# The rotary part of attention's scores as three pairs of 64-row products instead of two pairs of 128-row products

## The chip, the cores and the metric

The kernel runs on one core of one Trainium2 chip. The metric is the device time of one execution in microseconds; three executions of the kernel before took 3389.27 to 3390.84 us, with a median of 3389.57 us.

## The reference, cut to what matters

Two decoder blocks follow each other over 1024 tokens of width 1024. The first has two layers (`DEPTH = 2`), each with latent attention, a convolution branch and a mixture of experts; the second block has other mixers and no such attention. The change lies in the attention of the two layers of the first block.

```
SEQ = 1024; N_ATTN_HEADS = 4; QK_NOPE_DIM = 128; QK_ROPE_DIM = 64; Q_BLOCK = 128

k_r = jnp.broadcast_to(k_rope[:, :, None, :], (B, S, N_ATTN_HEADS, QK_ROPE_DIM))
k = jnp.concatenate([k_nope, k_r], axis=-1)
q = rms_norm(q, q_head_g)
k = rms_norm(k, k_head_g)
q = jnp.concatenate([q[..., :QK_NOPE_DIM], apply_rope(q[..., QK_NOPE_DIM:], cos, sin)], axis=-1)
k = jnp.concatenate([k[..., :QK_NOPE_DIM], apply_rope(k[..., QK_NOPE_DIM:], cos, sin)], axis=-1)
def attend(q_blk):
    s = jnp.einsum('bhqd,bhkd->bhqk', q_blk, kt, preferred_element_type=jnp.float32) * scale
    p = jax.nn.softmax(s, axis=-1).astype(vt.dtype)
    return jnp.einsum('bhqk,bhkd->bhqd', p, vt)
```

A head's key has 192 numbers: 128 without position and 64 that are rotated. Scores, softmax and output are computed for blocks of 128 queries.

## The kernel before, in words

Five engines run programs written out by hand; they are ordered only by the semaphores that the code names. Each layer runs `project`, then `heads`, then `attend`, then `conv_norm_and_mix`, then the experts.

**Scores (`scores`, L1207 to L1217).** For a head and a block of 128 queries, TensorE fills two PSUM banks, one for each half of the 1024 keys (512 keys a half). Values are kept as a rounded part and a remainder (`_hi`, `_lo`), so that products can run in the faster fp32r form. The 128 position-free rows take three products for each half: high by high, high by low, low by high. The 64 rotated rows are laid out so that they fill 128 rows: `k_parts` holds the keys' high part in rows 0 to 63 and their low part in rows 64 to 127, and the queries (`qs_rope_hi`, `qs_rope_lo`) stand twice, once in each half of the rows. Two products for each half do these: the high queries with both key parts, and the low queries with both. This makes ten products of 128 rows for a call of `scores`.

**The loop (`attend`, L1243 to L1262).** There are 8 query blocks by 4 heads, 32 calls of `scores` in a layer and 64 in all. For head g TensorE turns the probabilities (8 transposes, `turn_probs`), computes the scores of head g + 2 (`scores`), and multiplies the probabilities of head g with the values (`outputs`, L1239, 8 products in plain fp32, which a trace shows as 16 records). VectorE meanwhile runs for each head the maximum over the scores (L1307), its scaling (L1309), the reciprocal of the row sum (L1314), the normalising of the probabilities (L1316), and taps of the convolution: one for each head (L1329) and a second one on every other head (L1335). ScalarE takes the exponential (L1268) and copies the turned probabilities. Two calls of `scores` stand ahead of the loop.

**The keys' rotary parts (`heads`).** In `heads` the keys of head h lie in `k_rope[:, h, :]`, the same 64 rotated rows twice. `scale_keys` on VectorE writes them. ScalarE's `rope_parts` (L923) rounds the upper 64 rows into scratch (`rope_hi` of that function, a row of `mix`) and the lower 64 rows into `k_parts`, each over 1024 keys; VectorE's `rope_low` (L976) subtracts the scratch from the upper rows. From the second head on ScalarE first waits until VectorE is done with the scratch (`rope_split`). `k_parts` lies in the same memory as `k_rope`.

**Order at the end of `heads`.** VectorE's queue holds, in this order, the scaling of the last head's keys (L973, L974), `rope_low` (L979), the splits of the position-free keys (L1016, L1018, L983), and the query scales (L1021 to L1025). ScalarE's queue holds `rope_parts`, `take` for the last query tile (L906, L907), `root` (L917) and `high` (L921). TensorE ends with products made to keep it busy (L223) and the transposes of L1056, whose moving part is 40 rows by 40 columns.

Of the kernel before, what the change touches and what calls it, by code (L numbers as in the profile page):

```python
# [13 lines left out]
F32 = mybir.dt.float32  # L14
# [118 lines left out]
def build(nc, A):  # L133
# [3 lines left out]
    with ExitStack() as top:  # L137
# [42 lines left out]
        def bank(i):  # L180
            return psum[:, i, :]
# [193 lines left out]
        def half_of(n):  # L375

            return slice(n * HALF, (n + 1) * HALF)
# [231 lines left out]
        def project(l, lcols, modl, gain, lc, shift, lat, y, mix, q):  # L609

            with ExitStack() as ctx:
# [15 lines left out]
                with nc.Block() as block:  # L627
# [137 lines left out]
                    def _(pe):  # L765
# [43 lines left out]
                        lat_spreads(1)  # L809
                        tile(conv_pairs[3], 1)  # L810

        def heads(l, lc, lat, q, y, mix):


# [4 lines left out]
            with ExitStack() as ctx:  # L819
# [6 lines left out]
                sum_rows = [slice(32 * half, 32 * half + 2 * HEADS) for half in range(2)]  # L826
                both_sums = slice(0, 32 + 2 * HEADS)
                row_roots = (mix[:, 3, 0:HALF], mix[:, 2, 0:HALF])
                rope_hi = mix[ROPE:P, 3, :].bitcast(F32R)
                cos_row = k_rope[:, HEADS - 1, :]  # L830

                rope_rows = [lat[:, 3, :], q_rope[:, 0, :], q_rope[:, 1, :]]
                names = ("w_in", "sq_done", "lat_done", "summed", "prod", "raw_done", "v_prod", "v_copied", "row_root", "root_turned", "rstd",
                         "spread_done", "q_scaled", "cos_part", "sin_part", "roped", "k_done", "rope_rounded",
                         "parts", "hi_rounded", "hi_after", "k_split", "rope_split", "conv_step")
                (w_in, sq_done, lat_done, summed, prod, raw_done, v_prod, v_copied, row_rooted, root_turned, inverted,
                 spread_done, q_scaled, cos_part, sin_part, roped, k_done, rope_rounded,
                 parts_done, hi_rounded, hi_after, k_split, rope_split, conv_step) = [sem("hd_" + n) for n in names]
                zeroed = sem("hd_zeroed")
                staged = [sem(f"hd_staged{p}") for p in range(HEADS // 2)]  # L840
                turned = [sem(f"hd_turned{n}") for n in range(3)]
# [13 lines left out]
                with nc.Block() as block:  # L855
# [43 lines left out]
                    @block.scalar  # L899
                    def _(act):  # L900
                        def take(n):
                            kind, j = tiles[n]
                            act.wait_ge(prod, n + 1)
                            if n:
                                act.wait_ge(summed, n)
                            act.activation(sq[:, (n + 1) % 2, :], banks(2 * (n % 2)), ACT.Square).then_inc(sq_done, 1)  # L906
                            act.activation(dest[kind][:, j, :], banks(2 * (n % 2)), ACT.Copy, scale=lc(gains[kind])).then_inc(raw_done, 1)  # L907

                        def copy_v(t):
                            act.wait_ge(v_prod, t + 1)  # L910
                            act.copy(v[:, t, :], bank(t % 4)).then_inc(v_copied, 1)

                        def root(i, count):
                            act.wait_ge(summed, count)
                            for half in range(2):
                                rows = sum_rows[half]
                                act.activation(row_roots[i][rows, :], bank(6 + half)[rows, :], ACT.Sqrt, bias=EPS,  # L917
                                               scale=1.0 / QK).then_inc(row_rooted, 1)

                        def high(h):  # L920
                            act.copy(k_hi[:, h, :], k_nope[:, h, :]).then_inc(hi_rounded, 1)  # L921

                        def rope_parts(i):  # L923
                            h = turn_order[i]
                            act.wait_ge(k_done, 2 * i + 2)
                            if i:
                                act.wait_ge(rope_split, i)
                            act.copy(rope_hi, k_rope[ROPE:P, h, :]).then_inc(rope_rounded, 1)
                            act.copy(k_parts[0:ROPE, h, :], k_rope[0:ROPE, h, :]).then_inc(parts_done, 1)

                        act.activation(sq[:, 0, :], lat[:, 3, :], ACT.Square).then_inc(sq_done, 1)
                        for n in range(n_k):
                            take(n)
                        root(0, 1 + n_k)
                        for t in range(TB):
                            copy_v(t)
                        rope_parts(0)
                        high(turn_order[0])
                        take(n_k)
                        rope_parts(1)  # L940
                        take(n_k + 1)
                        rope_parts(2)
                        take(n_k + 2)
                        take(n_k + 3)
                        take(n_k + 4)
                        rope_parts(3)
                        take(n_k + 5)
                        root(1, 1 + len(tiles))
                        act.wait_ge(k_done, 2 * HEADS)
                        high(turn_order[3])  # L950

                    @block.vector
                    def _(dve):
# [21 lines left out]

                        def rope_low(i):  # L976
                            h = turn_order[i]
                            dve.wait_ge(rope_rounded, i + 1)
                            dve.tensor_tensor(k_parts[ROPE:P, h, :], k_rope[ROPE:P, h, :], rope_hi.bitcast(F32), ALU.subtract).then_inc(rope_split, 1)  # L979

                        def low(h, n):
                            dve.wait_ge(hi_rounded, n)
# [137 lines left out]
        def attend(l, lc, y, mix, q):  # L1120
# [8 lines left out]
            with ExitStack() as ctx:  # L1129
# [30 lines left out]
                with nc.Block() as block:  # L1160
# [12 lines left out]
                    @block.gpsimd  # L1173
                    def _(pool):
                        def stage(pair, count, at):

                            two = slice(2 * pair, 2 * pair + 2)
                            loaded, rounded = (pool.snap(pool.to_reg(n)) for n in (64 * (count - 1), 4 * count - 2))
                            pool.tensor_copy(qs_hi[:, two, :], q_nope[:, two, at]).then_inc(staged[pair], 1)
                            pool.wait_ge(rope_loaded[pair], 64)  # L1180
                            pool.wait_ge(rope_loaded[pair], loaded)
                            pool.tensor_copy(rope_hi[:, two, :], rope_in[:, two, :]).then_inc(staged[pair], 1)
                            pool.wait_ge(staged[pair], 2)
                            pool.wait_ge(staged[pair], rounded)
                            pool.tensor_tensor(qs_lo[:, two, :], q_nope[:, two, at], qs_hi[:, two, :].bitcast(F32),
                                               ALU.subtract).then_inc(staged[pair], 1)
                            pool.tensor_tensor(rope_lo[:, two, :], rope_in[:, two, :], rope_hi[:, two, :].bitcast(F32),
                                               ALU.subtract).then_inc(staged[pair], 1)

                        for pair in range(HEADS // 2):  # L1190
                            pool.sem_inc(staged[pair], 4)
                        with pool.Fori(0, last_blk) as blk:
                            nxt = blk + 1

                            pool.wait_ge(conv_step, n_conv * blk + 1)
                            pool.wait_ge(more_step, ATTEND_MORE * blk + 1)
                            pool.tensor_copy(taps[:, 0:n_conv], lc("conv_w")[:, bass.ds(n_conv * blk + first_tap, n_conv)]).then_inc(taps_in, 1)
                            pool.tensor_copy(taps[:, n_conv:n_conv + ATTEND_MORE],
                                             lc("conv_w")[:, bass.ds(ATTEND_MORE * blk + first_more, ATTEND_MORE)]).then_inc(taps_in, 1)
                            for pair in range(HEADS // 2):  # L1200

                                pool.wait_ge(scores_done, HEADS * blk + 2 * pair + 2)
                                stage(pair, blk + 2, bass.ds(nxt * P, P))

                    @block.tensor
                    def _(pe):
                        def scores(h, slot, blk):  # L1207

                            pe.wait_ge(staged[h // 2], 4 * blk + 4)

                            parts = ((qs_hi[:, h, :], k_hi[:, h, :]), (qs_hi[:, h, :], k_lo[:, h, :]), (qs_lo[:, h, :], k_hi[:, h, :]),
                                     (rope_hi[:, h, :], k_parts[:, h, :]), (rope_lo[:, h, :], k_parts[:, h, :]))
                            for n, (queries, keys) in enumerate(parts):
                                for half in range(2):
                                    mm = pe.matmul(bank(2 * slot + half), queries, keys[:, half * HALF:(half + 1) * HALF],
                                                   start=n == 0, stop=n == len(parts) - 1)
                            mm.then_inc(scores_done, 1)  # L1217

                        for b in range(2):
                            pe.sem_inc(pv_done[b], 1)  # L1220
# [82 lines left out]
                    @block.vector  # L1303
                    def _(dve):
                        def maxima(h, slot, g, blk):
                            dve.wait_ge(scores_done, g + 1)
                            dve.reduce_max(row_max[:, slot:slot + 1], score_slot(slot), AX.X).then_inc(maxes, 1)  # L1307
                            dve.wait_ge(maxes, g + 1)
                            dve.tensor_scalar(neg_max[:, slot:slot + 1], row_max[:, slot:slot + 1], q["q_neg"][:, h, blk], None,  # L1309
# [2491 lines left out]
```

## Time and profile before

| | us |
|---|---|
| median of 3 executions | 3389.57 |
| the profiled execution | 3392.0 |
| its span, first to last instruction | 3390.2 |
| TensorE busy (share of the span) | 3253.7 (96%) |
| VectorE busy | 2698.2 (80%) |
| ScalarE busy | 1805.7 (53%) |
| GpSimd busy | 695.2 (21%) |
| mean granted clock of TensorE | 0.987 |

The attention loops of the two layers stand at 254 to 411 us and at 1375 to 1532 us of the span. The other numbers that matter are the starts of TensorE's products: matmuls are pipelined, so the time that one costs is the distance to the start of the next, and not its duration. In a timeline, rows of the same line and tiles that follow each other are put together, with their count; the distance between the starts of two such rows, divided by the count of the first, is the pace.

### The profile page before, as it was taken

The numbers are of one execution on the slowest core, as the hardware profiler recorded it, in microseconds if no ns is written. First come the engines' busy times: TensorE is split into PE (matmuls) and PEld (weight loads), VectorE is DVE, ScalarE is ACT, GpSimd is POOL, SyncE is SP. The second block draws the span as 40 slices with busy tenths as digits, with TensorE's granted clock in tenths as the row PEclk, the third lists the DMA queues.
The fourth block names the chain that finished last, engine by engine and source line by source line (L and its number), as shares of the span: only waits on it lengthen the run. The fifth ranks groups of instructions, "written<-read, shape, count | busy, mean of one in ns | idle before, by whom it ended". The sixth has DMA issues, their size and how long they took to land. (4 is left out here: it accounts for less than half of the span.)

```text
span 3390.2 us, 43771 instructions
## 1 busy us (share of the span) xinstructions
PE 3253.7 (96%) x15518; PEld 2613.1 (77%) x15518; DVE 2698.2 (80%) x2480; ACT 1805.7 (53%) x1929; POOL 695.2 (21%) x552
## 2 busy tenths in 40 slices
PE   6999997999999999999799999999998999999998
PEld 3859884888888786797578888878777878888786
DVE  6988887888888788888788888876744488888677
ACT  5254444888888634544378888863333353434223
POOL 0213200111111020320011111104443023233232
PEclk9999998999999999999899999999999999999999
DMA  5120067999999412005599999962110434454853
GB/s 199 38 87 22 17 219 275 394 398 392 398 389 401 165 44 90 22 10 174 193 354 391 400 387 400 391 239 100 52 38 13 149 109 158 137 167 149 360 237 137
DMA packets 143519, 703.09 MB, mean 207 GB/s; under 512 B 19376, under 2 KB 28080, under 8 KB 90672
## 3 DMA queue, kind: packets, MB, share of 16 engines
q1 hardware_dynamic: 132240, 664.65, 51.2%
q0 software_dynamic: 8928, 32.51, 3.6%
q10 hardware_dynamic: 2240, 4.46, 0.3%
q8 instruction: 69, 1.13, 0.1%
q14 instruction: 42, 0.34, 0.0%
HBM read 608.75 MB, written 85.46 MB: 205 GB/s over the span
## 5 line engine op out<-in xcount | busy, mean ns | idle before, releaser
L2168 DVE TENSOR_TENSOR ex_lo_layer<-mix_layer,ex_hi_layer 128x2048 fp32r<-128x2048 f32 x128 | 291.7, 2290 | 23.1 <-ACT ex_hi_layer L2102 21.0
L2168 DVE TENSOR_TENSOR ex_lo<-mix,ex_hi 128x2048 fp32r<-128x2048 f32 x128 | 291.6, 2289 | 22.5 <-ACT ex_hi L2102 21.3
L2102 ACT CAST ex_hi_layer<-mix_layer 128x2048 fp32r<-128x2048 f32 x126 | 240.9, 1912 | 64.0 <-PE psum L2022 50.7
L2102 ACT CAST ex_hi<-mix 128x2048 fp32r<-128x2048 f32 x126 | 240.6, 1910 | 52.2 <-PE psum L2022 50.9
L3124 PE MATMUL psum<-ff_rest,w_hi 128*128 128x512 f32 x776 | 241.3, 392 | 10.2 <-DVE ff_ev L3402 3.8
L2020 PE MATMUL psum<-ex_hi,xe_hi 128*128 128x512 f32 x512 | 201.5, 394 | 1.0 <-DVE xe_lo L2173 1.0
L2020 PE MATMUL psum<-ex_hi_layer,xe_hi_layer 128*128 128x512 f32 x512 | 201.4, 393 | 1.0 <-DVE xe_lo_layer L2173 1.0
L2022 PE MATMUL psum<-ex_hi_layer,xe_lo_layer 128*128 128x512 f32 x512 | 200.1, 391 | 0.0
L2022 PE MATMUL psum<-ex_hi,xe_lo 128*128 128x512 f32 x512 | 199.9, 390 | 0.0
L2021 PE MATMUL psum<-ex_lo,xe_hi 128*128 128x512 f32 x512 | 199.8, 390 | 0.0
L2021 PE MATMUL psum<-ex_lo_layer,xe_hi_layer 128*128 128x512 f32 x512 | 199.8, 390 | 0.0
L3124 PEld LDWEIGHTS psum<-ff_rest,w_hi 128*128 128x128 f32 x776 | 145.6, 189 | 44.0 <-issue 8.6
L3124 PE MATMUL psum<-ff_rest,ff_a_hi 128*128 128x512 f32 x512 | 158.9, 392 | 1.5 <-DVE ff_rest L3541 1.5
L3124 PE MATMUL psum<-ff_rest,w_lo 128*128 128x512 f32 x388 | 151.9, 391 | 0.0
L496 PE MATMUL psum<-xn_hi,w_hi 128*128 128x512 f32 x384 | 120.0, 394 | 1.7 <-DVE xn_lo L2269 1.2
L603 DVE SCALAR_TENSOR_TENSOR mix_layer<-y_layer,lcols,mix_layer 128x1024 f32<-128x1024 f32 x79 | 118.5, 1502 | 2.6
L603 DVE SCALAR_TENSOR_TENSOR mix<-y,lcols,mix 128x1024 f32<-128x1024 f32 x79 | 118.2, 1499 | 2.6
L496 PE MATMUL psum<-xn_lo,w_hi 128*128 128x512 f32 x384 | 118.3, 389 | 0.0
L496 PE MATMUL psum<-xn_hi,w_lo 128*128 128x512 f32 x384 | 118.2, 389 | 0.0
L3124 PEld LDWEIGHTS psum<-ff_rest,ff_a_hi 128*128 128x128 f32 x512 | 96.6, 189 | 22.5 <-DVE ff_rest L3541 1.9
L2020 PEld LDWEIGHTS psum<-ex_hi_layer,xe_hi_layer 128*128 128x128 f32 x512 | 96.6, 189 | 20.8 <-issue 1.3
L2020 PEld LDWEIGHTS psum<-ex_hi,xe_hi 128*128 128x128 f32 x512 | 96.5, 189 | 20.7 <-issue 1.3
(763 smaller groups left out, 8883.2 us busy)
## 6 DMA issues: line engine op xcount, KB each, us to landing
mix<-w_experts_dram SPq DMA_DIRECT2D x128, 1024.0 KB, 7.5
mix_layer<-w_experts_dram SPq DMA_DIRECT2D x128, 1024.0 KB, 7.3
first_w<-w_experts_dram SPq DMA_DIRECT2D x64, 1024.0 KB, 8.2
hid_rows<-x SPq DMA_DIRECT2D x71, 512.0 KB, 3.7
ex_raw<-w_experts_dram SPq DMA_DIRECT2D x32, 1024.0 KB, 7.8
ex_raw_layer<-w_experts_dram SPq DMA_DIRECT2D x32, 1024.0 KB, 7.6
first_w<-w_in_dram SPq DMA_DIRECT2D x42, 512.0 KB, 3.2
ff_rest<-hid_rows SPq DMA_DIRECT2D x13, 1536.0 KB, 14.7
```

The source lines that it names most:

```text
L496: mm = pe.matmul(bank(out + half), wt, xt[:, half * HALF:(half + 1) * HALF], start=first and n == 0, stop=last and n == 2)
L603: dve.scalar_tensor_tensor(out=acc, in0=y[:, j, t:t + S], scalar=lc("conv_w")[:, j * TAPS_PAD + t:j * TAPS_PAD + t + 1], in1=acc, op0=ALU. ...
L2020: pe.matmul(bank(out), x_hi, h[:, k, :], start=first, stop=False)
L2021: pe.matmul(bank(out), x_hi, r[:, k, :], start=False, stop=False)
L2022: mm = pe.matmul(bank(out), x_lo, h[:, k, :], start=False, stop=end)
L2102: act.copy(hi[j % PARTS][:], raw[j % RAW][:]).then_inc(w_hi, 1)
L2168: dve.tensor_tensor(lo[j % PARTS][:], raw[j % RAW][:], hi[j % PARTS][:].bitcast(F32), ALU.subtract).then_inc(w_lo, 1)
L3124: mm = pe.matmul(out, wt[:, k, :], xt(k), start=fresh and k == 0 and j == 0, stop=k == kt - 1 and j == 2, skip_group_check=True)
```

## The change

The rotary products contract 64 rows each. `rope_tiles` gives, for the first half of the keys, rows 0 to 63, and for the second half, rows 64 to 127, and in those rows the place of the high and of the low part of the keys. In `k_parts`, the low part of a half of the keys stays in the columns of that half, and the high part goes to the columns of the other half. Three products are made for each half (high by high, high by low, low by high; the product of the two low parts falls away), six of 64 rows in place of four of 128 rows. They alternate between the upper and the lower rows of the array and between two PSUM banks. In the built program each of them carries an array tile of 64 rows by 128 columns, at row 0 or at row 64; the other products of `scores` carry one of 128 by 128. The transposes of L1056 carry a tile of 64 by 128 already before, those of L1049 tiles of 128 by 32 at columns 0 and 32, and those of L2651 one of 128 by 64.

In `heads` the scratch row and the wait for `rope_split` go: ScalarE rounds 64 rows by 512 keys twice, straight into `k_parts`, and VectorE subtracts 64 rows by 512 keys twice. `scores_done` is counted twice for a call, and its waits are doubled.

```diff
+        def rope_tiles(k_parts, h):
+
+            return [(group, k_parts[group, h, half_of(1 - half)], k_parts[group, h, half_of(half)])
+                    for half, group in enumerate((slice(0, ROPE), slice(ROPE, P)))]
...
                         def rope_parts(i):
                             h = turn_order[i]
                             act.wait_ge(k_done, 2 * i + 2)
-                            if i:
-                                act.wait_ge(rope_split, i)
-                            act.copy(rope_hi, k_rope[ROPE:P, h, :]).then_inc(rope_rounded, 1)
-                            act.copy(k_parts[0:ROPE, h, :], k_rope[0:ROPE, h, :]).then_inc(parts_done, 1)
+                            for half, (group, hi, _) in enumerate(rope_tiles(k_parts, h)):
+                                act.copy(hi, k_rope[group, h, half_of(half)]).then_inc(rope_rounded, 1)
...
                         def rope_low(i):
                             h = turn_order[i]
-                            dve.wait_ge(rope_rounded, i + 1)
-                            dve.tensor_tensor(k_parts[ROPE:P, h, :], k_rope[ROPE:P, h, :], rope_hi.bitcast(F32), ALU.subtract).then_inc(rope_split, 1)
+                            for half, (group, hi, lo) in enumerate(rope_tiles(k_parts, h)):
+                                dve.wait_ge(rope_rounded, 2 * i + half + 1)
+                                dve.tensor_tensor(lo, k_rope[group, h, half_of(half)], hi.bitcast(F32), ALU.subtract).then_inc(rope_split, 1)
...
-                                pool.wait_ge(scores_done, HEADS * blk + 2 * pair + 2)
+                                pool.wait_ge(scores_done, 2 * HEADS * blk + 4 * pair + 4)
...
-                            parts = ((qs_hi[:, h, :], k_hi[:, h, :]), (qs_hi[:, h, :], k_lo[:, h, :]), (qs_lo[:, h, :], k_hi[:, h, :]),
-                                     (rope_hi[:, h, :], k_parts[:, h, :]), (rope_lo[:, h, :], k_parts[:, h, :]))
+                            parts = ((qs_hi[:, h, :], k_hi[:, h, :]), (qs_hi[:, h, :], k_lo[:, h, :]), (qs_lo[:, h, :], k_hi[:, h, :]))
                             for n, (queries, keys) in enumerate(parts):
                                 for half in range(2):
-                                    mm = pe.matmul(bank(2 * slot + half), queries, keys[:, half * HALF:(half + 1) * HALF],
-                                                   start=n == 0, stop=n == len(parts) - 1)
-                            mm.then_inc(scores_done, 1)
+                                    pe.matmul(bank(2 * slot + half), queries, keys[:, half_of(half)], start=n == 0, stop=False)
+                            halves = rope_tiles(k_parts, h)
+                            for queries, part in ((rope_hi, 1), (rope_hi, 2), (rope_lo, 1)):
+                                for half in range(2):
+                                    group, keys = halves[half][0], halves[half][part]
+                                    mm = pe.matmul(bank(2 * slot + half), queries[group, h, :], keys, start=False, stop=queries is rope_lo)
+                                    if queries is rope_lo:
+                                        mm.then_inc(scores_done, 1)
...
-                            dve.wait_ge(scores_done, g + 1)
+                            dve.wait_ge(scores_done, 2 * g + 2)
```

On TensorE, in the attention loop, the order stands like this before; the names are tiles (`first_w` holds the turned probabilities there, `const` the identity, `y` the probabilities), and the size is that of the output:

```order
L1231 MATMUL psum<-const,y 128x128 x8
L1209 REGISTER_ALU
L1215 MATMUL psum<-k_hi,qs_hi 128x512 x2
L1215 MATMUL psum<-k_lo,qs_hi 128x512 x2
L1215 MATMUL psum<-k_hi,qs_lo 128x512 x2
L1215 MATMUL psum<-k_parts,qs_rope_hi 128x512 x2
L1215 MATMUL psum<-k_parts,qs_rope_lo 128x512 x2
L1235 ISA
L1238 REGISTER_ALU
L1239 MATMUL psum<-first_w,v 128x128 x8
```

and like this in the changed kernel:

```order
L1238 MATMUL psum<-const,y 128x128 x8
L1212 REGISTER_ALU
L1217 MATMUL psum<-k_hi,qs_hi 128x512 x2
L1217 MATMUL psum<-k_lo,qs_hi 128x512 x2
L1217 MATMUL psum<-k_hi,qs_lo 128x512 x2
L1222 MATMUL psum<-k_parts,qs_rope_hi 128x512 x4
L1222 MATMUL psum<-k_parts,qs_rope_lo 128x512 x2
L1242 ISA
L1245 REGISTER_ALU
L1246 MATMUL psum<-first_w,v 128x128 x8
```

Two products of 128 rows with `qs_rope_hi` became four of 64 rows, the two with `qs_rope_lo` now have 64 rows, and nothing else moved.

On VectorE, at the end of `heads` of the first layer, before:

```order
L973 TENSOR_TENSOR k_nope<-k_nope,psum 128x1024
L974 TENSOR_TENSOR k_rope<-lat,psum 128x1024
L979 TENSOR_TENSOR k_parts<-k_rope,mix 64x1024
L1016 TENSOR_SCALAR k_hi<-k_nope 128x1024
L1018 TENSOR_TENSOR k_lo<-k_nope,k_hi 128x1024
```

and in the changed kernel:

```order
L975 TENSOR_TENSOR k_nope<-k_nope,psum 128x1024
L976 TENSOR_TENSOR k_rope<-lat,psum 128x1024
L982 TENSOR_TENSOR k_parts<-k_rope,k_parts 64x512 x2
L1019 TENSOR_SCALAR k_hi<-k_nope 128x1024
L1021 TENSOR_TENSOR k_lo<-k_nope,k_hi 128x1024
```

The one subtraction over 1024 keys is now two over 512 keys in the same place.

## Rows read from the trace of the kernel before

**Rows 1.** The page's part 1: busy time of each engine.
```profile
PE 3253.7 (96%) x15518; PEld 2613.1 (77%) x15518; DVE 2698.2 (80%) x2480; ACT 1805.7 (53%) x1929; POOL 695.2 (21%) x552
```

**Rows 2.** Windows, attention: busy PE, PEld, DVE, ACT, POOL, then PEclk.
```profile
254.00:408.00 154.00, 153.98 (x1038) 140.44 (x1039) 130.51 (x170) 75.32 (x152) 45.86 (x70) 1.00 0.06 16
```

**Rows 3.** Who waited for whom there: us in total, times, longest.
```profile
DVE row_max L1307 <- PE psum L1215: 10.4, 12, 3.2
```

**Rows 4.** Timeline, first layer: two heads, start us, us from start to end.
```profile
282.02 0.71 PE L1215 MATMUL psum<-k_hi,qs_hi 128*128 128x512 f32 x2
...
283.48 0.61 PE L1215 MATMUL psum<-k_parts,qs_rope_hi 128*128 128x512 f32 x2
...
283.93 0.62 PE L1215 MATMUL psum<-k_parts,qs_rope_lo 128*128 128x512 f32 x2
...
284.39 1.95 PE L1239 MATMUL psum<-first_w,v 128*128 128x128 f32 x16
284.59 1.23 DVE L1307 TENSOR_REDUCE row_max<-psum 128x1 f32<-128x1024 f32 x1 [0.16 <-PE psum L1215]
...
286.17 1.04 PE L1231 MATMUL psum<-const,y 128*128 128x128 f32 x8
...
286.96 0.71 PE L1215 MATMUL psum<-k_hi,qs_hi 128*128 128x512 f32 x2
```

**Rows 5.** The same timeline, PE in `heads`: products of 128 rows without a change of tile.
```profile
219.24 7.03 PE L1040 MATMUL psum<-lat,first_w 128*128 128x512 f32 x16
226.11 1.04 PE L394 MATMUL psum<-const,hd_rstd 128*128 128x128 f32 x8
```

**Rows 6.** The same, to tiles of 128 by 32 (L1049) and back.
```profile
238.15 3.60 PE L1040 MATMUL psum<-lat,first_w 128*128 128x512 f32 x8
241.68 1.03 PE L1049 MATMUL psum<-mix,const 128*8 128x512 f32 x4
242.64 3.70 PE L1040 MATMUL psum<-lat,first_w 128*128 128x512 f32 x8
246.27 1.03 PE L1049 MATMUL psum<-mix,const 128*8 128x512 f32 x4
```

**Rows 7.** The same, to a tile of 64 by 128 (L1056) and back.
```profile
211.46 1.98 PE L1066 MATMUL psum<-k_rope,lat 128*128 128x512 f32 x4
213.37 0.44 PE L1056 MATMUL psum<-const,mix 40*128 40x40 f32 x4
213.74 1.13 PE L1066 MATMUL psum<-k_rope,lat 128*128 128x512 f32 x2
214.70 1.04 PE L394 MATMUL psum<-const,hd_rstd 128*128 128x128 f32 x8
```

**Rows 8.** Timeline of the second block: back from a tile of 128 by 64 (L2651).
```profile
2590.29 1.16 PE L2676 MATMUL psum<-v_t,ke_t 128*128 128x128 f32 x8
2591.28 1.02 PE L2683 MATMUL psum<-hc_sq,const 128*128 128x512 f32 x2
```

**Rows 9.** Timeline, the start and end of the first layer's attention.
```profile
256.57 1.22 DVE L1307 TENSOR_REDUCE row_max<-psum 128x1 f32<-128x1024 f32 x1 [3.21 <-PE psum L1215]
...
258.85 1.23 DVE L1307 TENSOR_REDUCE row_max<-psum 128x1 f32<-128x1024 f32 x1 [0.80 <-PE psum L1215]
...
407.89 1.95 PE L1239 MATMUL psum<-first_w,v 128*128 128x128 f32 x16
...
409.32 1.22 DVE L1307 TENSOR_REDUCE row_max<-psum 128x1 f32<-128x1024 f32 x1
```

**Rows 10.** Timeline, the end of `heads` on VectorE and ScalarE.
```profile
245.63 1.22 DVE L979 TENSOR_TENSOR k_parts<-k_rope,mix 64x1024 fp32r<-64x1024 f32 x1 [1.11 <-ACT mix L928]
...
244.56 1.04 ACT L928 CAST mix<-k_rope 64x1024 fp32r<-64x1024 f32 x1 [0.74 <-DVE k_rope L974]
```

**Rows 11.** Groups of instructions by line: casts and subtractions of 512 columns.
```profile
L3449 DVE TENSOR_TENSOR x<-x 128x512 fp32r<-128x512 f32 x71 | 46.9, 684 | 0.0
...
L3190 ACT CAST ff_a_hi<-ff_s 128x512 fp32r<-128x512 f32 x44 | 26.9, 616 | 0.7
```

More of the change, by code:

```diff
@@ L828, in heads @@
                 row_roots = (mix[:, 3, 0:HALF], mix[:, 2, 0:HALF])
-                rope_hi = mix[ROPE:P, 3, :].bitcast(F32R)
                 cos_row = k_rope[:, HEADS - 1, :]
@@ L834, in heads @@
                          "spread_done", "q_scaled", "cos_part", "sin_part", "roped", "k_done", "rope_rounded",
-                         "parts", "hi_rounded", "hi_after", "k_split", "rope_split", "conv_step")
+                         "hi_rounded", "hi_after", "k_split", "rope_split", "conv_step")
                 (w_in, sq_done, lat_done, summed, prod, raw_done, v_prod, v_copied, row_rooted, root_turned, inverted,
                  spread_done, q_scaled, cos_part, sin_part, roped, k_done, rope_rounded,
-                 parts_done, hi_rounded, hi_after, k_split, rope_split, conv_step) = [sem("hd_" + n) for n in names]
+                 hi_rounded, hi_after, k_split, rope_split, conv_step) = [sem("hd_" + n) for n in names]
                 zeroed = sem("hd_zeroed")
```

## The prediction

> **What bounds the kernel now.** First the page's part 1: TensorE (PE) is busy for 96% of the span, VectorE (DVE) for 80% [rows 1]. That is an average over stages, so the second view is the windows view of the one stage that the change touches most. In the first layer's attention loop PE is busy for 153.98 of 154.00 us, DVE for 130.51, at a granted clock of 1.00 [rows 2]. Third, who waits for whom there: DVE waits for the scores (`row_max` <- PE) 10.4 us in all [rows 3], and 3.21 and 0.80 us of it are the two waits at the start [rows 9], so 6.4 us are left in the loop. PE waits for nobody. The period of a head, from one `scores` to the next, is 286.96 - 282.02 = 4.94 us [rows 4], and it is made of PE's own work. So a nanosecond more or less in `scores` moves the end by as much, down to the point at which DVE's own work sets the period: 6.4 us over 31 heads, or 0.21 us a head, below now. The second layer has the same program and starts 1121 us later.
>
> **What PE pays for a product.** Starts count, not durations. The last four rotary products run from 283.48 to 284.39, 0.227 us each [rows 4], and they are fp32r products of 512 columns. The fp32 products of `heads` (L1040), which serve as a scale below, start 0.429 us apart: 16 in 6.87 us [rows 5].
>
> **What the change takes away.** Of ten products in a call of `scores` four go (4 x 0.227 = 0.908 us). Six of 64 rows come. If the two of a pair, in different rows of the array and in different banks, run at the same time, three pairs cost 3 x 0.227 = 0.681 us and a call gains 0.227. If they don't, six cost 1.362 us and a call loses 0.454. The trace has no fp32r product of 64 rows. The nearest rows are L1049: four records, two each for column tiles 0 and 32, go from 241.68 to 242.64, 0.96 us [rows 6]. One after the other they would take 4 x 0.429 = 1.72 us; two at a time 0.86, and 0.10 us is left over, which is the next term. So tiles of this kind do run side by side here, with two streams of moving data. I take that for the row tiles too, with 0.007 us for the start of the second, which is what 0.96 leaves when the next term's 0.095 and two paces are taken off, and keep the other end for a rival.
>
> **What the change adds: a change of tile on the way in and on the way out.** The view is the timeline of PE around the few products that have another tile than 128 by 128. Eight products of L1040 with nothing odd around them are 8 x 0.429 = 3.43 us. The eight that stand before L1049 take 241.68 - 238.15 = 3.53: 0.10 more (0.095 before rounding), between the last of them and the first product of the other tile. The eight that have L1049 on both sides take 246.27 - 242.64 = 3.63 [rows 6]: another 0.10, which is the first weight load, of 128 columns, that no longer lies under the product ahead. The tile of 64 by 128, the very one that the change uses, shows the same. L1066 has four products between L1049 and L1056, from 211.46 to 213.37: 1.91 us against 1.72, 0.19 for one load and one drain. After L1056 two products take 214.70 - 213.74 = 0.96 us against 0.86, 0.10 for the load alone [rows 7]. For the product that follows in the loop (`outputs`, plain fp32, 128 columns) the row is L2676: after a tile of 128 by 64 eight records take 0.99 us [rows 8], while 16 of `outputs` take 286.17 - 284.39 = 1.78, or 0.89 for eight [rows 4]: again 0.10.
>
> So a call of `scores` pays 0.095 + 0.10 on the way in (before the first 64-row product, which needs a load of 128 columns too) and 0.095 + 0.10 on the way out (before `outputs`), 0.39 us. For three of the four parts rows of the same kind stand above. The load on the way in has none in fp32r: it may be hidden (0), if a load for the new tile can run ahead, or cost 0.21, if the loads of the two row groups stand in line; I take 0.10, since after both changes to a 128-by-128 tile it was bare and only once [rows 6, 7].
>
> **Sum for a call:** -0.227 + 0.007 + 0.39 = +0.170 us. Bounds by the load: +0.07 and +0.28.
>
> A word on the notes. The trace shows two tiles at a time for a price of one product and 0.10 us for each change of tile. The Trainium skill (TensorE: Matmul & The Clock Gate, Part 3, "The mechanism") says that weight loads for another row group are pulled ahead of products in flight, and gives the span of a pack as one product plus about 4 ns a tile; it puts no price on going from the full array to the pack. By that rule a call would gain some 0.22 us. The same section measured 3.07 times for four row tiles of 512 columns, not four; an estimate from this would make a pair dearer than one product. No row here has row tiles side by side, so neither can be tested on this trace.
>
> **How many calls count.** 64 calls, 32 a layer. The two ahead of the loop count: DVE waits for each [rows 9]. The last of a layer does not: its products end by about 408.1 (the next line's start at 407.89 and 0.2), while DVE gets to its maximum only at 409.32 [rows 9], so 1.2 us of slack swallow 0.17. That makes 62 calls: 62 x 0.170 = 10.5 us. Nothing behind hides it: what follows waits for the end of attention, and DMA in that stage stands at 0.06 of its capacity [rows 2].
>
> **The keys in `heads`.** DVE's subtraction of 1024 columns costs 1.22 us [rows 10]; one of 512 columns 0.684 [rows 11], and two in a row, whose starts stand closer than that, about 1.3. Three of the four in a layer stand in a queue that does not wait, and cost 0.1 each. The fourth waits 1.11 us for ScalarE (ACT), whose first copy takes 1.04 [rows 10]; with a copy of 512 columns at 0.616 [rows 11] DVE starts 0.4 us earlier, and its second half follows without a wait. Together 0.3 - 0.4 = -0.1 us a layer. ACT's two copies fall from 2.1 to 1.2 us, and without the wait for `rope_split` it is earlier at places where PE does not wait for it. Bounds: -0.4 and +0.3 a layer. I take -0.2 us for both. GpSimd and DMA issues are untouched. The doubled count of `scores_done` adds an increment to a product and no instruction.
>
> **The time.** 3392.0 (profiled) + 10.5 - 0.2 = 3402.3. The profiled execution stands 2.4 us above the median of the runs shown; on the median it is 3389.6 + 10.3 = 3399.9.
>
> **The rivals.**
> 1. *The first load on the way in is hidden* (+0.07): 62 x 0.07 = 4.3, less 0.2: 3393.7. For it: the new tile's load needs only half the array. Against: after both changes back it is bare [rows 6, 7]. Chance 0.09.
> 2. *The two row groups' loads stand in line* (+0.28): 17.1, 3406.7. For it: every product still has a load of its own of 128 columns, and loads of L1049 have only 8. Chance 0.08.
> 3. *Not slower: the changes of tile cost next to nothing here*, because the pairs interleave with the products around them as the notes' rule has it. Then a call gains 0.22 us, and DVE's slack of 0.21 a head just allows it: 62 x 0.21 = 13.0 us less, 3376.4. It decides where the two changes cost less than the one product saved: 0.22 for both, against 0.39 in the rows. For it: nothing in the trace has fp32r beside a tile change. Against: rows 6 to 8, three tiles of different form, one price. Chance 0.11.
> 4. *The change does not do what it says*: the pairs don't overlap, because each member writes all 128 partitions of its bank and the column tiles of L1049 write few. Then 6 x 0.227 against 4 x 0.227, and 0.39: +0.84 a call, 52 us, 3441.6. Chance 0.09.
>
> **How the numbers follow.** The forecast has 0.63; its own range is 3396 to 3404 (each of the four parts off by 0.01 to 0.02, and `heads`). A measurement of this kernel can tell about 0.2%, 6.8 us, from no change. Of the 0.63, 0.07 lie below +6.8 us. Slower: 0.56 + 0.08 + 0.09 = 0.73; same: 0.07 + 0.09 = 0.16; faster: 0.11. The range leaves out rivals 3 and 4 (0.20 together), takes in 1 and 2 with their bounds from `heads`: 3392.5 to 3408.
>
> **What would show it.** In the changed kernel's timeline of PE: the second product of a pair starts within some 0.01 us of the first (else rival 4); pairs start 0.23 us apart; from the last `k_hi,qs_lo` to the first `k_parts,qs_rope_hi` some 0.32 us instead of 0.227 and a first pair longer by 0.10 (less: rival 1; 0.2: rival 2); after the last pair 0.32 us to `outputs`, whose first product is longer by 0.10. The period of a head goes from 4.94 to 5.11, PE stays busy all through, and DVE's wait for the scores grows from 10.4 us by about 5 us a layer. A period below 4.94 would make the forecast wrong; so would a lower granted clock in the loop, which is 1.00 now.

## The result and the profile after

The changed kernel takes 3397.44 us (median of 20 runs, 3394.29 to 3401.81), the kernel before beside it 3388.81 us (20 runs): a ratio of 1.0027, with a 95% interval of 1.0020 to 1.0033. It is slower, by 8.6 us, with an interval of 6.8 to 11.2 us. On another occasion the same kernel stood at 3400.00 us against 3388.93, ratio 1.0031 (1.0020 to 1.0042). Medians are of the fast runs alone: one run of that occasion took 3934.67 us at a granted clock of 0.79, and one of a later experiment 5537.43 us at 0.56, both left out. The profiled execution of the changed kernel took 3397.19 us, with a span of 3395.4 us.

The busy time of the engines, from the profile page of the changed kernel, says almost nothing of it; it answers [rows 1]:

```profile
PE 3262.2 (96%) x15646; PEld 2589.4 (76%) x15646; DVE 2698.5 (79%) x2488; ACT 1799.7 (53%) x1929; POOL 706.3 (21%) x552
```

The timeline of TensorE (PE) in the loop of the changed kernel, columns as in [rows 4] (start us, us to the end, engine, line, tiles, form, count):

```profile
281.69 0.70 PE L1217 MATMUL psum<-k_hi,qs_hi 128*128 128x512 f32 x2
282.23 0.63 PE L1217 MATMUL psum<-k_lo,qs_hi 128*128 128x512 f32 x2
282.69 0.63 PE L1217 MATMUL psum<-k_hi,qs_lo 128*128 128x512 f32 x2
283.25 0.73 PE L1222 MATMUL psum<-k_parts,qs_rope_hi 64*128 64x512 f32 x4
283.82 0.40 PE L1222 MATMUL psum<-k_parts,qs_rope_lo 64*128 64x512 f32 x2
284.14 2.05 PE L1246 MATMUL psum<-first_w,v 128*128 128x128 f32 x16
286.03 1.04 PE L1238 MATMUL psum<-const,y 128*128 128x128 f32 x8
286.83 0.70 PE L1217 MATMUL psum<-k_hi,qs_hi 128*128 128x512 f32 x2
```

The period of a head is 286.83 - 281.69 = 5.14 us; it was 4.94 [rows 4]. Take it in three parts. The six products of 128 rows last from 281.69 to 283.25: 1.56 us, against 1.46 before (282.02 to 283.48). The rotary products last from 283.25 to 284.14: 0.89 us against 0.91, so six 64-row products cost almost as much as the four of 128 rows that they replace. `outputs` lasts from 284.14 to 286.03: 1.89 us against 1.78. The transposes are as they were (0.80 and 0.79).

So what was added sits around the small tile. Before it 0.10 us in which no product starts; in it 0.21 us beyond three paces of 0.227; behind it 0.11 us in the first product of `outputs`. VectorE (DVE) sees it as waiting. Who waited for whom, 254 to 413 us, against [rows 3]:

```profile
DVE row_max L1314 <- PE psum L1222: 16.0, 16, 3.8
```

In the same stretch PE is busy for 159.00 of 159.00 us, at a granted clock of 1.00 as before.

For a whole layer I take the time from the first product of `scores` to the first centring of the convolution's rows, which ends the stage. Kernel before: 254.02 to 414.00, 159.98 us. Changed: 252.67 to 418.14, 165.47 us. These are the last two of those rows, from the timelines of PE and of DVE of the changed kernel:

```profile
252.67 0.70 PE L1217 MATMUL psum<-k_hi,qs_hi 128*128 128x512 f32 x2 [1.33 <-PEq L859]
...
418.14 2.35 DVE L1384 SCALAR_TENSOR_TENSOR mix<-psum,mix 128x1024 f32<-128x1024 f32 x2 [0.89 <-PE psum L1264]
```

That is +5.49 us; the second layer has +5.46, together +10.95. This measure is more exact than the time of a whole run. From their first product to their last, the experts of a layer took 541.2 us in some profiles and 539.6 in others, also between two profiles of the same kernel, and the start of the program moved by up to 3.5 us; the two profiles of the changed kernel differ by 3.7 us in their spans and by 0.03 in this stage.

### The profile page after: what moved, and what is told of

Its sections match the earlier page's. It is cut to its first block and busy times, and to the rows that moved or that the text cites. A ratio compares the mean times of both kernels' runs of the same rounds, so it can differ in the third digit from the quotient of the medians.

```text
span 3395.4 us, 44085 instructions
## 1 busy us (share of the span) xinstructions
PE 3262.2 (96%) x15646; PEld 2589.4 (76%) x15646; DVE 2698.5 (79%) x2488; ACT 1799.7 (53%) x1929; POOL 706.3 (21%) x552
```

## The experiments

All times of a stage are the measure just described, both layers; the kernel before has 159.98 and 160.01 us.

### The changed kernel once more, and the keys alone

> The changed kernel once more, on the same chip as its neighbours here, as the yardstick for them: 8 to 11 us above before.

Measured: 3400.00 against 3388.93 us, +11.1 (interval 6.8 to 14.2), at the upper edge of what was expected. Stages 165.50 and 165.49: +11.0 us.

> Only the other part of the change: the keys' rotary parts are rounded and subtracted in the new layout in heads, and the scores are made with the old ten products of 128 rows, which read that layout as if it were the old one (the rotary term of the scores is therefore another one). Theory (TensorE's way through heads ends with GpSimd's staging of the queries, which the change leaves alone): 0 us, within 0.5 us of before. Rival (VectorE and ScalarE end the stage, as the prediction had it, and give back 0.1 to 0.5 us a layer): 0.2 to 1 us below before. The two differ by less than the clocking can tell, so the trace decides: the time from the first product of heads to the first of attention, 56.92 us before.

The edit, against the changed kernel:

```diff
-                            parts = ((qs_hi[:, h, :], k_hi[:, h, :]), (qs_hi[:, h, :], k_lo[:, h, :]), (qs_lo[:, h, :], k_hi[:, h, :]))
+                            parts = ((qs_hi[:, h, :], k_hi[:, h, :]), (qs_hi[:, h, :], k_lo[:, h, :]), (qs_lo[:, h, :], k_hi[:, h, :]),
+                                     (rope_hi[:, h, :], k_parts[:, h, :]), (rope_lo[:, h, :], k_parts[:, h, :]))
...
-                            for queries, part in ((rope_hi, 1), (rope_hi, 2), (rope_lo, 1)):
```

Measured: 3387.91 against 3388.93 us, ratio 1.0000 (0.9991 to 1.0009). Stages 160.02 and 160.02 us, the same as before. From the first product of `heads` to the first of attention it took 56.93 and 56.80 us; the kernel before took 56.92 and 56.93. The whole loss is in the scores, and the new keys give between 0 and 0.13 us a layer. The timeline of the end of `heads` shows why it is not more. Before (the first product of attention starts at 254.02):

```profile
251.53 1.70 POOL L896 TENSOR_TENSOR qs_rope_lo<-qs_rope,qs_rope_hi 128x256 fp32r<-128x256 f32 x1
...
253.19 0.17 DVE L1025 TENSOR_SCALAR q_neg<-hd_rstd 128x32 f32<-128x32 f32 x1
```

and in the changed kernel, where the first product of attention starts at 252.67:

```profile
251.24 0.77 POOL L900 TENSOR_TENSOR qs_rope_lo<-qs_rope,qs_rope_hi 128x256 fp32r<-128x256 f32 x1
...
251.25 0.17 DVE L1028 TENSOR_SCALAR q_neg<-hd_rstd 128x32 f32<-128x32 f32 x1
```

These rows are of the first layer. In the second layer of the same execution `heads` starts at 1320.96 and attention at 1377.76:

```profile
1375.29 1.70 POOL L900 TENSOR_TENSOR qs_rope_lo_layer<-qs_rope_layer,qs_rope_hi_layer 128x256 fp32r<-128x256 f32 x1
...
1376.96 0.18 DVE L1028 TENSOR_SCALAR q_neg_layer<-hd_rstd_layer 128x32 f32<-128x32 f32 x1
```

Counted from the first product of `heads` (197.10 before; 195.73 and 1320.96 now), VectorE ended at 56.3 us before and ends at 55.7 and 56.2 now. GpSimd's staging of the queries ended at 56.1 before and ends at 56.3 and 56.0 now. VectorE was last by 0.13 us before. In the first layer of this trace GpSimd is last now, and nothing is gained; in the second VectorE is last again, and the stage is 0.13 us shorter.

The second layer is the usual case. With the old keys this stretch took 56.89 to 56.93 us in all eight layers that were traced; with the new keys it took 56.79 to 56.80 in ten of twelve, and 56.93 in the other two, both of them first layers. In those two VectorE's last subtraction took 1.23 us instead of 1.71, and GpSimd's first rounding (L894) 0.96 instead of 0.40; why the two engines fared differently there is not shown. So the new keys give about 0.12 us a layer, the low end of what the rival said. The theory (0 us, as GpSimd ends the stage) fits the two odd layers alone.

### A change of tile alone, and the same small product without one

> The kernel before with one small product added at the end of each call of scores, 64 rows by 8 columns, in a tile of 64 by 128; it adds a rotary term a second time to 8 columns of the scores, so the scores of those columns are off. Theory (each change of tile drains the array, about 0.10 us, and lays the next weight load of 128 columns bare, about 0.10 us): 0.10 + 0.105 + 0.10 + 0.10 and about 0.03 for the product, 0.43 us a call, 27 us above before, 3416 us; period 5.37. Rival (what costs in the changed kernel is that there are more products and loads, not the tile): as much as the same small product with 128 rows costs in the next run.

> As the run before, with the small product over 128 rows by 8 columns, so in the same 128-by-128 tile as its neighbours; the scores of 8 columns are off in the same way. Theory: its own load lies under the product ahead, the load of the product behind (128 columns, 0.107 us) is what its slot lasts: +0.11 us a call, 7 us above before, 3396 us; period 5.05. Rival (products and loads cost, not the tile): 0.4 us a call here too, 3416 us.

The edit, against the kernel before, with `0:ROPE` in the first and `:` in the second:

```diff
-                                                   start=n == 0, stop=n == len(parts) - 1)
+                                                   start=n == 0, stop=n == len(parts) - 1 and half == 1)
+                            mm = pe.matmul(psum[:, 2 * slot, 0:8], rope_hi[0:ROPE, h, :], k_parts[0:ROPE, h, 0:8], start=False, stop=True)
                             mm.then_inc(scores_done, 1)
```

Measured: with the tile 3412.67 us against 3388.22, +24.5 (ratio 1.0068, 1.0051 to 1.0085); without it 3396.94, +8.7 (1.0024, 1.0014 to 1.0033). Stages: 172.46 and 172.45 with the tile (+24.9), 163.48 and 163.49 without (+7.0). Periods 5.38 and 5.07 us. The timeline of PE, first with the 64-row tile:

```profile
300.81 0.61 PE L1215 MATMUL psum<-k_parts,qs_rope_lo 128*128 128x512 f32 x2
301.36 0.27 PE L1217 MATMUL psum<-k_parts,qs_rope_hi 64*128 64x8 f32 x1
301.56 2.05 PE L1240 MATMUL psum<-first_w,v 128*128 128x128 f32 x16
303.44 1.04 PE L1232 MATMUL psum<-const,y 128*128 128x128 f32 x8
```

then with the same product over 128 rows:

```profile
301.90 0.61 PE L1215 MATMUL psum<-k_parts,qs_rope_lo 128*128 128x512 f32 x2
302.35 0.17 PE L1217 MATMUL psum<-k_parts,qs_rope_hi 128*128 128x8 f32 x1
302.38 2.03 PE L1240 MATMUL psum<-first_w,v 128*128 128x128 f32 x16
304.25 1.04 PE L1232 MATMUL psum<-const,y 128*128 128x128 f32 x8
```

With the tile the two products ahead of it take 301.36 - 300.81 = 0.55 us instead of 0.45: 0.10 in which nothing starts. The small product then lasts 0.20 until `outputs` (0.10 drain, and its own load of 0.10), and `outputs` 1.88 instead of 1.78. These rows hold 0.40 us of the 0.44 by which the period grew, for a product that computes next to nothing; its twin in the tile of its neighbours costs 0.13. The two edits differ only in the rows of the small product, and with them in its tile; that difference costs 0.31 us. That it is not the 64 rows as such, the next experiment shows. Both theories held: the periods were expected at 5.37 and 5.05 us, and of the 27 and 7 us expected for the whole the stages show 24.9 and 7.0. The rival, that more products and loads cost as such, would have them equal; it falls. That the array drains when the tiling changes is also what the Trainium skill has (TensorEngine Tiling (Array Packing), Key Properties: "Mode switching requires drain"); the page has no figure, and here it is 0.10 us each way, with a load of 0.10 us behind each that nothing covers.

### Half as many changes of tile

> The changed kernel with half as many changes of tile: on even heads the six 128-row products, then the six 64-row products of this head and, straight behind them in the same tile, the six of the next head (they open its banks, after TensorE has waited for the exponential that last read them); on odd heads only the six 128-row products are left. The same products in all, one stay in the small tile for two heads. Theory (the loss is the two changes, 0.41 us a stay, measured in the changed kernel's trace): 0.20 us less a head than the changed kernel, 31 x 2 heads: 12.6 us below it, 3385 us, and level with the kernel before within 2 us; mean period 4.93. Rival (the loss lies in the pairs themselves, as each is dearer than a product of 128 rows): no gain over the changed kernel, 3397 us.

The edit, against the changed kernel; `full` and `rotary` are the two halves of `scores`:

```diff
+                        def scores(h, slot, blk, g):
+                            if h % 2 == 0:
+                                full(h, slot, blk, True)
+                                rotary(h, slot, False)
+                                if g is not None:
+                                    pe.wait_ge(exp_done, g + 2)
+                                rotary(h + 1, 1 - slot, True)
+                            else:
+                                full(h, slot, blk, False)
```

Measured: 3389.83 us against 3388.93, ratio 1.0002 (0.9993 to 1.0011), and 10.2 us below the changed kernel beside it. Stages 159.91 and 159.89 us: 11.2 us below the changed kernel (12.6 were expected), and 0.2 below the kernel before, as expected. Timeline of PE on an even head, whose stay in the small tile has six pairs:

```profile
291.98 0.73 PE L1226 MATMUL psum<-k_parts,qs_rope_hi 64*128 64x512 f32 x4
292.55 0.40 PE L1226 MATMUL psum<-k_parts,qs_rope_lo 64*128 64x512 f32 x2
292.79 0.62 PE L1226 MATMUL psum<-k_parts,qs_rope_hi 64*128 64x512 f32 x4
293.25 0.40 PE L1226 MATMUL psum<-k_parts,qs_rope_lo 64*128 64x512 f32 x2
293.57 2.05 PE L1260 MATMUL psum<-first_w,v 128*128 128x128 f32 x16
```

The second head's three pairs start 0.23 us apart and pay no drain and no bare load: 292.79, and the way out at 293.57 is 0.78 us later (3 x 0.227 and 0.10). The rival, that the pairs themselves are too dear, falls. The pairs do save a product for each head; two changes of tile for two heads cost 0.41 us, and two saved products are 0.45; in the loop two heads take 9.87 us together, against 2 x 4.94 = 9.88 before. That is level with the kernel before, and no gain worth its extra order.

### Do the pairs need to stand side by side in the program?

> The changed kernel with its six 64-row products in another order: the three of rows 0 to 63 first, then the three of rows 64 to 127. Same work, same tile, the same two changes of tile. Theory (two products overlap only when they follow each other in different row groups and banks): only the third and the fourth overlap, five paces of 0.23 us instead of three, +0.46 us a call, 62 calls: 28 us above the changed kernel, about 3426 us, and a head's period of 5.60 us. Rival (64-row products are cheap whatever their rows, as each fills half the array): no difference from the changed kernel, 3397 us, period 5.14.

```diff
-                            for queries, part in ((rope_hi, 1), (rope_hi, 2), (rope_lo, 1)):
-                                for half in range(2):
+                            for half in range(2):
+                                for queries, part in ((rope_hi, 1), (rope_hi, 2), (rope_lo, 1)):
```

Measured: 3399.48 us against 3388.22, ratio 1.0028 (1.0019 to 1.0038). Stages 165.71 and 165.69 us: the changed kernel's 165.47 within 0.24. My theory fell; its 28 us are not there. The order in the program is now, for a call, high, high, low of the first half and then high, high, low of the second. The timeline of PE in that kernel shows another:

```profile
281.14 0.74 PE L1222 MATMUL psum<-k_parts,qs_rope_hi 64*128 64x512 f32 x4
281.71 0.40 PE L1222 MATMUL psum<-k_parts,qs_rope_lo 64*128 64x512 f32 x2
282.05 2.05 PE L1246 MATMUL psum<-first_w,v 128*128 128x128 f32 x16
```

Four with the high queries, then two with the low: the fourth product of the program started 0.01 us after the first. All 64 calls in the trace show this order. The two row groups are served side by side, each in its own order.

> The run with two heads together, its twelve 64-row products in another order: the six of rows 0 to 63 (three of each head) first, then the six of rows 64 to 127. In the earlier run three and three ran side by side although they stood one group after the other. Theory (each row group takes its products from what is queued, at least six products of the other group further on): again six pairs, stage time from the first scores to the centring within 1 us of 159.9 us a layer. Rival (it looks ahead only a few products, three being near its limit): up to three of the six run alone, 3 x 0.23 us for every two heads, 15.5 x 0.69 = 11 us a layer more, 171 us.

The edit, against the kernel with two heads together (`rotary` now makes one half):

```diff
-                                rotary(h, slot, False)
                                 if g is not None:
                                     pe.wait_ge(exp_done, g + 2)
-                                rotary(h + 1, 1 - slot, True)
+                                for half in range(2):
+                                    rotary(h, slot, False, half)
+                                    rotary(h + 1, 1 - slot, True, half)
```

Measured in a single run each: 3407.74 us against 3389.29. Stages 169.04 and 169.03 us, 9.1 a layer above the run with two heads together. Both theories are off; the rival was nearer (11). Timeline of PE:

```profile
293.94 0.73 PE L1225 MATMUL psum<-k_parts,qs_rope_hi 64*128 64x512 f32 x2
294.51 0.39 PE L1225 MATMUL psum<-k_parts,qs_rope_lo 64*128 64x512 f32 x1
294.52 0.85 PE L1225 MATMUL psum<-k_parts,qs_rope_hi 64*128 64x512 f32 x4
295.09 0.51 PE L1225 MATMUL psum<-k_parts,qs_rope_lo 64*128 64x512 f32 x2
295.32 0.62 PE L1225 MATMUL psum<-k_parts,qs_rope_hi 64*128 64x512 f32 x2
295.78 0.39 PE L1225 MATMUL psum<-k_parts,qs_rope_lo 64*128 64x512 f32 x1
296.10 2.05 PE L1260 MATMUL psum<-first_w,v 128*128 128x128 f32 x16
```

Two products start alone. The third, of the low queries, starts at 294.51, and one of the high queries 0.01 us later; in these traces two products of the same rows never start closer than 0.22 us, so this is the seventh of the program, the first of the other rows. The two groups then run side by side, out of step, and the last products are alone again. The seventh did not start beside the first or the second, six and five places ahead of it, but beside the third, four places ahead. A stay in the small tile lasts 2.16 us (293.94 to 296.10) instead of 1.59 (291.98 to 293.57), 0.57 more where the rival had 0.69; there are 16 a layer, which is the 9.1 us. All 32 stays of the trace have this order, with starts that agree within 0.01 us. The products of the other rows were not missing: TensorE's register step ahead of `outputs` (L1256), which stands behind all twelve in the program, ran at 293.45 in this call, half a microsecond before the first of them started.

### Where VectorE sets the period

> The kernel before without the two products of the low part of the rotary queries (the scores leave that term out): eight products a call, 0.454 us less, with no change of tile. It asks where VectorE's own work sets the period. From the prediction: VectorE's waits for the scores in the loop are 6.4 us a layer, 0.21 us a head, so TensorE's gain stops there: 13 us below before, 3376 us, period 4.73. Rival (VectorE's other waits shrink too, and TensorE stays the bound): 62 x 0.454 = 28 us below, 3361 us, period 4.49.

```diff
-                                     (rope_hi[:, h, :], k_parts[:, h, :]), (rope_lo[:, h, :], k_parts[:, h, :]))
+                                     (rope_hi[:, h, :], k_parts[:, h, :]))
```

Measured: 3372.63 us against 3388.22, ratio 0.9951 (0.9935 to 0.9968), -15.6 us; not the 28 of the rival. Stages 152.14 and 154.39 us, together -13.5. Who waited for whom, 260 to 395 us:

```profile
DVE row_max L1307 <- PE psum L1215: 0.5, 1, 0.5
```

VectorE hardly waits for scores any more and sets the pace, though it is busy for 121.55 of the 135 us: the rest is short waits, the largest for ScalarE's exponential and for its own maximum. Four heads in a row took 18.68 us there (301.12 to 319.80), 4.67 a head, and 4.72 in the second layer. So in the loop the slack below 4.94 was 0.27 and 0.22 us a head, not 0.21. The ends of the layers gave part of it back: from the last scores to the centring it took 9.84 and 10.84 us, against 8.48 before. What is left, 13.5 us, is what this run was expected to gain (13).

## Why the prediction was right, point by point

**The sign and the size.** Forecast 3399.9 us in a range of 3392.5 to 3408, measured 3397.4 and 3400.0. Against the kernel before, +10.3 was forecast; +8.6 and +11.1 were measured for whole runs, +10.95 for the two stages. That the sum is so close is in part luck: a call lost more than forecast, and fewer calls' worth of it reached the end. The reason given is the reason found: the first experiments put the loss in the scores alone, the small product puts it in the change of tile, and two heads in one stay take it back.

**What bounds the kernel.** Right: PE's period and the stage moved together in every run that made a call dearer.

**The pairs.** Right, from a row of another shape. L1049's column tiles in [rows 6] run side by side, and so do the row tiles: four with the high queries from 283.25 to 283.82 are 0.57 us, two paces: 0.34 with the bare load, and 0.23. Rival 4 (no overlap, +52 us) had no part.

**The changes of tile.** Right in all four parts, 0.02 too small together. Forecast for a call: 0.095 + 0.10 in, 0.095 + 0.10 out, -0.22 for the pairs: +0.170. The medians over 60 of the calls give 0.10 + 0.11 in and 0.095 + 0.105 out, 0.41 against 0.39. Measured in the three parts of the period: +0.10, -0.02 and +0.11; the median period of either layer grew from 4.940 to 5.137, +0.197. The load on the way in, for which no row of this form stood ahead, was once bare and not twice: 0.11. Rivals 1 and 2 had it at 0 and 0.21.

**How many calls count.** This step was off, and it offset the former. 62 calls at 0.197 would be 12.2 us; the stages show 10.95, so 56 calls' worth. At the start, VectorE's first wait for scores is 0.03 us longer than before, not 0.17, measured from the first product: the way out of the small tile comes after `scores_done`. From the first to the last `scores` of the loop a layer lost 5.93 us; at its end 0.44 us of it were taken in. There VectorE's queue is longer, by the additions of L1343 (L1350 in the changed kernel), and from its maximum for the last head but one on it sets the pace, no longer TensorE: from there to the centring it is 403.43 to 414.00 before and 407.56 to 418.14 now, 10.57 and 10.58 us. I had allowed for the last call alone, 0.17.

**The keys.** Right in the main: -0.1 us a layer was forecast, and 0.12 less was measured in ten of twelve layers. VectorE waits 0.68 us instead of 1.11 for ScalarE's first copy, as forecast (0.4 less), and counted from the start of `heads` it ends the last `rope_low` at 49.63 us instead of 49.75. The step that I left out is GpSimd's queue, which ends only 0.13 us ahead of VectorE: in the two odd layers it ended last and took the gain back.

**The rivals.** Rival 3 (changes of tile next to free, 3376 us) fell with the changes of tile at 0.41 us a call. Its bound on the gain, 0.21 us a head or 13 us in all, was borne out in the sum (13.5) by the run with two products fewer, though in the loop VectorE could run at 4.67 and 4.72.

## What to carry to other kernels

Two products of 64 rows and 512 columns in different halves of the array cost one, but going to that tile and back costs about 0.41 us here, nearly two products of 0.227: half of it is time in which nothing starts, half the first weight load, which nothing covers. So a stay in a small tile has to save about two such products before it gains anything; make stays long, over several heads or outputs, or leave the half-filled products in the full tile. The price can be read ahead from any place where the kernel already changes tile: compare the starts of the same products with and without the change beside them.

## What the runs showed of the hardware that I had not expected

Products for different row groups are not started in the order of the program. Three of the upper and three of the lower rows, one group after the other, took 0.90 us of PE as alternating ones did (0.89). With six and six, two started alone before the other group joined, which speaks against products that were put in pairs before the program ran. The Trainium skill (TensorE: Matmul & The Clock Gate, Part 3, "The mechanism") says of matmuls that they are "strict FIFO, no reordering"; the measurement decides, and here that does not hold across row groups. In that one kernel, run once, it reached four products ahead and not five, in all 32 stays; what sets that reach is open, and longer rows of one group were not tried.
